# Attention steps on one Trainium2 core: every second step in turned order, the reciprocals spread by GpSimd and turned once, the sign of the maximum changed by GpSimd

## The reference, cut to what matters

```
s = jnp.einsum('nbqhgd,nbkhd->nbhgqk', qb, kw) * (dh ** -0.5)      # scores, masked or biased
m = jnp.max(s, axis=-1)                                            # and the sink, if there is one
e = jnp.exp(s - m[..., None])
den = jnp.sum(e, axis=-1)                                          # + exp(sink - m)
o = jnp.einsum('nbhgqk,nbkhd->nbqhgd', e / den[..., None], vw)
```

## Time and profile before

| | us |
|---|---|
| median of 3 runs | 3315.79 |
| lowest, highest | 3314.12, 3320.33 |
| span of the profiled execution | 3318.4 |
| A units, from the first score to the last but for B | 525.9 to 578.4 |
| B units | 578.4 to 626.0 |
| `c` units | 1578.8 to 1645.0 |
| `ax` units | 2514.8 to 2570.0 |

### The profile page before, as it was taken

One profiled execution on the slowest core, in us unless ns is written; L12 is line 12 of the kernel. 1 busy time (PEld: TensorE's weight loads), 2 busy tenths in 40 slices (PEclk: granted clock), 3 DMA queues, 4 the chain that ended last, 5 costly groups with the idle time before them and its releaser, 6 DMA issues. The chain is left out here.

```text
span 3318.4 us, 46903 instructions
## 1 busy us (share of the span) xinstructions
PE 3219.3 (97%) x20286; PEld 2468.8 (74%) x20286; DVE 1527.3 (46%) x2217; ACT 1068.0 (32%) x1596; POOL 308.7 (9%) x365
## 2 busy tenths in 40 slices
PE   9999999999999999999999999979999999989988
PEld 7888887888888888889788888758877888434332
DVE  5443556644435544332754434685567544201112
ACT  4222226432224322222732223553344323200001
POOL 1000131200001000000300001211111301100000
PEclk9999999999999999999999999989999999999999
DMA  4222441122233222332222222301010323899998
GB/s 144 102 90 90 145 143 40 39 102 89 90 96 113 102 89 90 96 107 108 84 97 94 98 88 98 106 20 49 3 65 20 105 99 124 345 427 425 425 427 336
DMA packets 62799, 448.77 MB, mean 135 GB/s; under 512 B 8705, under 2 KB 10369, under 8 KB 32641
## 3 DMA queue, kind: packets, MB, share of 16 engines
q1 hardware_dynamic: 62592, 445.76, 35.9%
HBM read 438.39 MB, written 2.10 MB: 133 GB/s over the span
## 5 line engine op out<-in xcount | busy, mean ns | idle before, releaser
L569 DVE TENSOR_TENSOR w_lo<-slot,w_hi 128x2048 fp32r<-128x2048 f32 (+4 forms) x243 | 487.1, 2005 | 331.6 <-ACT w_hi L560 329.3
L167 PE MATMUL bank<-xa,w_hi 128*128 128x512 f32 x1368 | 535.9, 392 | 1.2 <-DVE w_lo L3170 1.1
L168 PE MATMUL bank<-xa,w_hi 128*128 128x512 f32 x1368 | 532.4, 389 | 0.0
L169 PE MATMUL bank<-xa,w_lo 128*128 128x512 f32 x1368 | 532.3, 389 | 0.0
L560 ACT ACTIVATE w_hi<-slot 128x2048 fp32r<-128x2048 f32 (+4 forms) x243 | 406.1, 1671 | 335.5 <-PE bank L169 326.3
L167 PE MATMUL bank<-xb,w_hi 128*128 128x512 f32 x832 | 324.7, 390 | 0.7 <-DVE w_lo L569 0.6
L168 PE MATMUL bank<-xb,w_hi 128*128 128x512 f32 x832 | 323.7, 389 | 0.0
L169 PE MATMUL bank<-xb,w_lo 128*128 128x512 f32 x832 | 323.7, 389 | 0.0
L167 PEld LDWEIGHTS bank<-xa,w_hi 128*128 128x128 f32 x1368 | 256.8, 188 | 63.1 <-issue 5.4
L169 PEld LDWEIGHTS bank<-xa,w_lo 128*128 128x128 f32 x1368 | 256.8, 188 | 53.8
L168 PEld LDWEIGHTS bank<-xa,w_hi 128*128 128x128 f32 x1368 | 256.8, 188 | 53.4 <-issue 1.2
(11 more groups left out here) (511 smaller groups left out, 4872.4 us busy)
## 6 DMA issues: line engine op xcount, KB each, us to landing
slot<-in_w_gu SPq DMA_DIRECT2D x87, 1024.0 KB, 4.7
slot<-in_exp_gate SPq DMA_DIRECT2D x25, 2048.0 KB, 15.2
slot<-in_exp_up SPq DMA_DIRECT2D x24, 2048.0 KB, 15.0
slot<-in_exp_down SPq DMA_DIRECT2D x24, 2048.0 KB, 15.8
slot<-in_w_dn SPq DMA_DIRECT2D x64, 704.0 KB, 4.0
slot<-in_w_gate SPq DMA_DIRECT2D x24, 768.0 KB, 4.3
xe<-in_exp_up SPq DMA_DIRECT2D x8, 2048.0 KB, 13.4
xe<-in_exp_down SPq DMA_DIRECT2D x8, 2048.0 KB, 15.2
```

The lines of the kernel that those rows point to most:

```text
L167: e.matmul(out, w[0], x[0], start=(j == 0), stop=False)
L168: e.matmul(out, w[0], x[1], start=False, stop=False)
L169: return e.matmul(out, w[1], x[0], start=False, stop=(j == n - 1))
L569: dve.e.tensor_tensor(lo, slot(k, b), hi.bitcast(F32), ALU.subtract).then_inc(L.up("w_lo", b))
```

## The change

Three edits, all in the attention functions.

1. TensorE: in a step with odd t whose S is narrow (or past the last unit), the order of the three parts is S(t), T(t-3), V(t-5); in the others it stays V, T, S. Since banks are taken in program order, the ring is walked in the new order too.
2. GpSimd writes the reciprocals of unit t-3 over 2 x 64 columns into a 128x128 tile (`inv_wide`, in `sqsum`, three slots), and TensorE transposes that tile once (called R' here) in place of the two matmuls R.
3. GpSimd negates the maximum of t-1 (`max_neg`) at the end of its step, in place of VectorE; the sink is taken less the maximum directly and no longer waits for the negated one.

```diff
+    def values(t):
...
-            pe.wait_ge(*L.at("den_inv", st, s))
-            for par in range(2):
-                inv = m.st[s % 6][:, 10 + par:11 + par].to_broadcast([P, 64])
-                last = e.matmul(bank[par * 64:par * 64 + 64, P:2 * P], inv, k.ident, start=True, stop=True)
-            last.then_inc(L.up("pv", st, s))
+        pe.wait_ge(*L.at("inv_wide", st, s))
+        e.transpose(bank[:, P:2 * P], tok(k.sqsum, s % 3), k.ident).then_inc(L.up("pv", st, s))
...
+        narrow = t >= n or len(units[t]["scores"][0]) == 1
+        order = ((scores, 0), (turns, 3), (values, 5)) if t % 2 and narrow else ((values, 5), (turns, 3), (scores, 0))
+        for part, late in order:
+            if 0 <= t - late < n:
+                part(t)
...
 def pool_attention(k, st, m, units):
-    for s in range(len(units)):
-        out = units[s]["out"]
-        pool.wait_ge(*L.at("att_scaled", st, s))
-        pool.e.tensor_copy(out[0], m.ot[s % 3]).then_inc(L.up("att_hi", st, s))
-        pool.wait_ge(*L.at("att_hi", st, s))
-        pool.e.tensor_tensor(out[1], m.ot[s % 3], out[0].bitcast(F32), ALU.subtract).then_inc(L.up("att_out", st, s))
+    n = len(units)
+    for t in range(n + 6):
+        if 0 <= t - 3 < n:
+            s = t - 3
+            inv = tok(k.sqsum, s % 3).rearrange("p (a c) -> p a c", a=2)
+            pool.wait_ge(*L.at("den_inv", st, s))
+            if s >= 3:
+                pool.wait_ge(*L.at("pv", st, s - 3))
+            pool.e.tensor_copy(inv, m.st[s % 6][:, 10:12].unsqueeze(2).to_broadcast([P, 2, 64])).then_inc(L.up("inv_wide", st, s))
+        if 0 <= t - 6 < n:
+            s = t - 6
...
+        if 0 <= t - 1 < n:
+            s = t - 1
+            stat, last = m.st[s % 6], len(units[s]["scores"][0]) - 1
+            pool.wait_ge(*L.at("max", st, s, last, 1))
+            pool.e.tensor_scalar(stat[:, 4:6], stat[:, 2 * last:2 * last + 2], -1.0, None, ALU.mult).then_inc(L.up("max_neg", st, s))
...
             dve.wait_ge(*L.at("max", st, s, last, 1))
-            e.tensor_scalar(stat[:, 4:6], stat[:, 2 * last:2 * last + 2], -1.0, None, ALU.mult).then_inc(L.up("max_neg", st, s))
             if u["sink"] is not None:
-                dve.wait_ge(*L.at("max_neg", st, s))
-                e.tensor_tensor(stat[:, 8:10], u["sinks"], stat[:, 4:6], ALU.add).then_inc(L.up("sink_less", st, s))
+                e.tensor_tensor(stat[:, 8:10], u["sinks"], stat[:, 0:2], ALU.subtract).then_inc(L.up("sink_less", st, s))
```

More of the change, by code:

```diff
@@ L861, in pe_attention @@
     n = len(units)
-    for t in range(n + 5):
[L863 to L873, removed]
-                for par in range(2):
-                    last = e.matmul(bank[par * 64:par * 64 + 64, 0:P], u["v"][par][j], tok(pt[par], j), start=(j == 0), stop=(j == nb - 1))
-            pe.wait_ge(*L.at("den_inv", st, s))
-            for par in range(2):
-                inv = m.st[s % 6][:, 10 + par:11 + par].to_broadcast([P, 64])
-                last = e.matmul(bank[par * 64:par * 64 + 64, P:2 * P], inv, k.ident, start=True, stop=True)
-            last.then_inc(L.up("pv", st, s))
[L881 to L910, removed]
@@ new lines, in values @@
+    def values(t):
+        s = t - 5
+        u, pt = units[s], m.pt[s % 2]
+        bank, freed = k.banks.take(("pv", st, s), ("att_scaled", st, s))
+        pe.wait_ge(*L.at(*freed))
+        pe.wait_ge(*L.at("probsT_a", st, s))
+        pe.wait_ge(*L.at("probsT_d", st, s))
+        for name in u["v_ready"]:
+            pe.wait_ge(*L.at(*name))
+        nb = len(u["v"][0])
+        for j in range(nb):
+            for par in range(2):
+                last = e.matmul(bank[par * 64:par * 64 + 64, 0:P], u["v"][par][j], tok(pt[par], j), start=(j == 0), stop=(j == nb - 1))
+        pe.wait_ge(*L.at("inv_wide", st, s))
+        e.transpose(bank[:, P:2 * P], tok(k.sqsum, s % 3), k.ident).then_inc(L.up("pv", st, s))
@@ new lines, in turns @@
+    def turns(t):
+        s = t - 3
+        nb = len(units[s]["v"][0])
+        for par in range(2):
+            pe.wait_ge(*L.at("exps", st, s, par))
+            for g in range(0, nb, 4):
+                bank, freed = k.banks.take(("turn", st, s, par, g), ("probsT_d" if par else "probsT_a", st, s, g))
+                pe.wait_ge(*L.at(*freed))
+                c = min(4, nb - g)
+                for j in range(c):
+                    last = e.transpose(tok(bank[:, :], j), tok(m.sc[s % len(m.sc)][par], g + j), k.ident)
+                last.then_inc(L.up("turned", st, s, par, g, also=[("turned", st, s, par)]))
@@ new lines, in scores @@
+    def scores(t):
+        u = units[t]
+        for name in u["ready"]:
+            pe.wait_ge(*L.at(*name))
+        for z in range(len(u["scores"][0])):
+            banks = []
+            for par in range(2):
+                bank, freed = k.banks.take(("scores", st, t, par, z), ("scores_out", st, t, par, z))
+                pe.wait_ge(*L.at(*freed))
+                banks.append(bank)
+            off = 0
+            for x in range(len(u["scores"][0][z])):
+                for par in range(2):
+                    q, keys = u["scores"][par][z][x]
+                    w = width(keys)
+                    last = e.matmul(banks[par][:, off:off + w], q, keys, start=True, stop=True)
+                off += w
+            last.then_inc(L.up("scores", st, t, z))
@@ L950, in pool_attention @@
     pool, L = k.pool, k.led
-    for s in range(len(units)):
-        out = units[s]["out"]
-        pool.wait_ge(*L.at("att_scaled", st, s))
-        pool.e.tensor_copy(out[0], m.ot[s % 3]).then_inc(L.up("att_hi", st, s))
-        pool.wait_ge(*L.at("att_hi", st, s))
-        pool.e.tensor_tensor(out[1], m.ot[s % 3], out[0].bitcast(F32), ALU.subtract).then_inc(L.up("att_out", st, s))
+    n = len(units)
+    for t in range(n + 6):
+        if 0 <= t - 3 < n:
+            s = t - 3
+            inv = tok(k.sqsum, s % 3).rearrange("p (a c) -> p a c", a=2)
[5 more added lines that the diff above has]
+            s = t - 6
+            out = units[s]["out"]
+            pool.wait_ge(*L.at("att_scaled", st, s))
+            pool.e.tensor_copy(out[0], m.ot[s % 3]).then_inc(L.up("att_hi", st, s))
+            pool.wait_ge(*L.at("att_hi", st, s))
+            pool.e.tensor_tensor(out[1], m.ot[s % 3], out[0].bitcast(F32), ALU.subtract).then_inc(L.up("att_out", st, s))
+        if 0 <= t - 1 < n:
[3 more added lines that the diff above has]
+            pool.e.tensor_scalar(stat[:, 4:6], stat[:, 2 * last:2 * last + 2], -1.0, None, ALU.mult).then_inc(L.up("max_neg", st, s))
 def dve_attention(k, st, m, units):
```

## The result

Five runs of each kernel on the same chip: before 3317.2 us (3314.1 to 3320.9), changed 3347.4 us (3337.8 to 3348.7). The ratio is 1.0081, with a 95% interval of 1.0069 to 1.0093: slower by 0.8%, where 0.46% was forecast and 3341 us was the upper end. The direction was right, the size half of what was measured.

What follows compares the result with a forecast made beforehand. TensorE was taken to bound attention before, bank-wait loops after the change; +3.0 (`c`), +3.0 (A), +10.1 (`ax`) and -0.9 (B) gave +15 us on the median, 3331 us, 0.46% slower, range 3318 to 3341.

Steps and rivals of the forecast that it cites:

- The bound before: In the attention stretches TensorE was taken as the bound, busy about 98% of the time at the full granted clock.
- TensorE's own time: In A, `c` and `ax`, the new order and single transpose were to save TensorE 0.27 us a pair, 0.13 a unit.
- The pair of 3.78: In `c`, two steps of TensorE's own work without bank waits: 4.05 less 0.27 us.
- The loops in `c` and A: Even S waits for the preceding S's banks, read by VectorE: pairs of 4.29 and 4.98 us, +3.0 us each stretch.
- the wake-up: TensorE's delay after its releaser in each loop, taken as ScalarE's 0.05 us, possibly up to 0.10 longer.
- The loop in `ax`: Even S waits for ScalarE's exponentials, two ScalarE steps: a pair of 8.70 us against 6.39, +10.1 us in all.
- TensorE's part: In `ax`, TensorE's work from the even S to the end of R', counted at 4.28 us a pair.
- VectorE's negation and GpSimd: In attention, GpSimd's spreading at 0.29 us and negation at 0.2 were to stay hidden; VectorE's saving counted nothing directly.
- TensorE stays the bound: Rival: banks free in time throughout attention, only TensorE's saving shows, 8.3 us faster, 3307.5 us; chance 0.08.
- Only `ax` waits: Rival: A and `c` gain, only the `ax` loop loses, +3 us, 3319 us; chance 0.10.
- GpSimd the bound: Rival: GpSimd's two new instructions at 0.74 us each set the pace in attention, 3344 us; chance 0.06.
- The sum: Whole kernel: 3.0 for `c`, 3.0 for A, 10.1 for `ax`, less 0.9 for B, +15 us.

Runs made afterwards that it cites:

- e7_inv: Kernel before with only the reciprocals spread by GpSimd and turned by one TensorE transpose: 3309.9 us, ratio 0.9973.
- e3_fill: Changed kernel plus twelve output-neutral transposes ahead of each even S of `ax` from step 6: 3337.0 us, 1.0058 of the kernel before.
- after: The changed kernel, all three edits made to the kernel before: 3347.4 us, ratio 1.0081.
- e8_neg: Kernel before with only the maximum's negation moved from VectorE to GpSimd: 3318.1 us, ratio 0.9998.
- e1_plain: Changed kernel with the order V, T, S in every step, both GpSimd edits kept: 3310.7 us, 0.9982 of the kernel before.
- e11_best: Changed kernel with odd narrow steps S, V, T and separate bank rings per kind in A and `c`, `ax` in old order: 3306.8 us, 0.9969 of before.
- e6_axonly: Changed kernel with the new order in `ax` alone, the old order elsewhere: 3329.7 us, 1.0033 of the kernel before.
- e10_svt: Changed kernel with V ahead of T in the reordered odd steps (S, V, T), one ring: 3321.2 us, 1.0012 of the kernel before.
- e9_turn: Kernel before with only the new TensorE order, both reciprocal matmuls and VectorE's negation kept: 3343.3 us, ratio 1.0078.

## Why the prediction was right in direction and half in size

**The bound before, and TensorE's own time.** Right. e7_inv shows the transpose's 0.11 a unit to the hundredth. The joint that adjoining S lose is there too: S, S and the gap to T take 1.08 in `c` against 1.06 counted, with no uncovered second load. The Trainium skill's rule on loads ("TensorE: Matmul & The Clock Gate", Part 3) would have made that 0.11 longer; the row doesn't show it, though both S use the same two halves of the rows, one for each head. The pair of 3.78 that the prediction counts for this order in `c` no run shows by itself, since S, T, V met a wait in every version.

**The loops in `c` and A.** Right in mechanism and nearly in size. In `c` the parts were 2.57 + 0.36 + 1.31 + 0.05 = 4.29. Measured are 2.58 (from S at 1613.46 to the end of R' at 1616.04), 0.35, 1.30 and 0.15: 4.38. In A a pair takes 5.12 against 4.98. The mis-sized term is the wake-up: the 0.05 of ScalarE was taken for TensorE, whose bound of "up to 0.10 longer" was the truth, 0.14 to 0.15 in both `c` and `ax`. In A the masks of 256 columns also start 0.40 apart, where 0.35 was taken. The whole of `ab` and `c` is 8.8 against the 5.1 of the terms (3.0 + 3.0 - 0.9); the loops' excess, 13 x 0.09 + 10 x 0.14, is 2.6 of the 3.7 between them. The rest, 1.1, is mostly at the starts, where S(5) waits before the count begins: S(6) starts 11.46 us after the first score of A (10.16 before) and 9.32 after that of `c` (8.58 before), so 1.30 and 0.74 are lost there, where 0.55 and 0.50 were counted.

**The loop in `ax`.** Right in mechanism, wrong by a factor of two: 10.1 predicted, 21.3 measured. The step that failed is TensorE's part, "4.28", whose durations were taken at the full clock of the earlier trace rows. The same prediction found that TensorE would stand idle for more than a quarter of each pair, and did not ask whether the clock would stay. It did not: TensorE's part is 5.99. e3_fill prices it at 8.3 us of the 11.2 missed. Some 3.2 us more are the stage's start. The prediction's count began at step 6, but S(4) and S(5) wait as well, as PE's timeline of after shows:

```profile
2530.28 1.13 PE L906 MATMUL bank<-kx,qx 64*128 64x512 f32 x4 [1.33 <-ACT scores L947]
2532.26 1.13 PE L906 MATMUL bank<-kx,qx 64*128 64x512 f32 x4 [0.85 <-ACT scores L947]
```

The first scaled output comes 13.5 us after the first score, against 10.2 before. What remains of the terms offsets itself: ScalarE's step took 1.98 rather than 2.10, the wake-up 0.14 rather than 0.05. That the full-clock pair came out at 8.66 against 8.70 is in this measure luck.

**VectorE's negation and GpSimd.** Right: the negation takes 0.219 us on GpSimd where 0.2 was taken, the spreading 0.290 where 0.29 was. The negation's move is without effect (e8_neg), and the plain order with both has no loss (e1_plain).

**The rivals.** "TensorE stays the bound" describes e1_plain and e11_best, without the turn or without the waits that it makes. The changed kernel rotates through the eight banks as the one before does, and loses time all the same. The rotation that the Trainium skill asks for ("Perfetto Trace Analysis", Optimizing Tensor Performance) is thus there in after too. The page does not call it sufficient, and these rows show that it isn't: what counts is who reads the bank last, and behind what. "Only `ax` waits" fell by the row at 1613.46, "GpSimd the bound" by e8_neg and e1_plain.

**The sum.** The forecast's 15.2 against 30.1: clock 8.3, start of `ax` 3.2, `ab` and `c` 3.7 make 15.2, over the 14.9 that was missed. No term of the sum had the clock in it, so the upper end, 3341, was too low by more than the wake-ups could mend. The fastest of the changed kernel's five runs, 3337.8 us, lies within the range, and its mean clock of 0.995 is among those of the kernel before (0.993 to 0.996 in the batches of the experiments): whether the range held went with how often the clock fell.

**Open.** Why the clock falls in some executions and not in others is not settled. In the profiled executions of after and e6_axonly every pair of S in the steady loop was slowed (3.6 to 3.7 us and 3.3 to 3.5, against 1.99), in e10_svt's one, in e9_turn's none, with idle stretches that are alike. That e9_turn's other runs mostly had the drop, and after's fastest run mostly not, is inferred from their time and their mean clock. That mean is over the whole kernel, and a stretch that the change does not touch (2180 to 2300 us) has 0.90 to 0.94 in every kernel looked at, so it does not say where the clock fell.

## What to carry to other kernels

Where buffers come from one ring, the order of issue decides who waits for whom: count back as many takes as there are buffers, name the reader of that one, and follow what this reader is queued behind. If the way leads back to the moved work, it is a loop, and its length, not the engine's busy time, is the period. End the stretch ahead of the readers with what they wait for (e10: V before T), and give each kind its own buffers where its readers differ (e11).

When a count finds a new idle stretch on TensorE, price the work behind it at half the clock too, and let the range reach to that.

## What the runs showed of the hardware

- The granted clock fell from 2.4 to 1.2 GHz around the two S behind a wait of 1.5 us, in a loop that waits so once in each pair of steps, with 0.24 us ahead of T: eight instructions took 3.68 us instead of 1.99, and the clock's mean over a pair was 0.83 (after). With 1.5 us of transposes in the place of the wait it didn't fall (e3_fill). At nearly the same waits, 1.45 us, it stayed up in e9_turn's profiled execution.
- The slow clock goes straight into the period here, since ScalarE is idle meanwhile: the two S take 3.68 us rather than 1.99, and the pair 10.35 rather than 8.66 (after, e3_fill).
- TensorE started 0.14 to 0.15 us after the end of the instruction that released it, on VectorE as on ScalarE (after, 1617.69 to 1617.84 and 2560.58 to 2560.72); ScalarE started 0.03 to 0.05 after TensorE's end, which the profile models.
- A change of kind on TensorE (S, T, V) costs a gap of about 0.10 us and an uncovered load of 0.05 to 0.11 by the earlier trace rows, S behind S nothing. e11_best, with one change less, gains 0.2 us a pair in `c` (3.64 against 3.84).
